# Small matmuls in blocks behind the weight units, and contractions filled up to 128 rows, in a two-layer decoder trunk

## What is computed

```python
h = rms_norm(x, norm1_g); proj = h @ w_in          # q,k,v,gates of three branches
log_a = log_sigmoid(ga @ gla_a_up + gla_a_b) / 16  # ga has 16 columns (LOWRANK)
# per chunk of 32 tokens (prompt) or per sequence of 8 (sample), for 4 GLA and 4 retention heads:
scores = where(causal, q_dec @ k_dec.T, 0)
o = q_dec @ S + scores @ v
S = exp(b_last) * S + k_end.T @ v                   # state update
# memory attention, 4 heads of 128 over 256 rows: the prompt shares one memory, each sample has its own cache
o_xa = softmax(q @ mem_k.T / sqrt(128)) @ mem_v
merged = sum(gate_b * (o_b @ w_br_b)); x = x + merged @ w_out
x = x + (gelu(conv(a)) * b) @ w_down                # a, b = h2 @ w_up
```

## Time and profile before

| | us |
|---|---|
| median of 3 runs | 1315.72 |
| the profiled execution, its own time | 1318.94 |
| span of that execution, first to last instruction | 1317.1 |
| TensorE matmul busy | 1273.7 (97% of the span) |
| GpSimd busy | 762.4 (58%) |
| VectorE busy | 641.3 (49%) |
| ScalarE busy | 578.5 (44%) |
| mean granted TensorE clock | 0.976 |

### The profile page before, as it was taken

One profiled execution on the slowest core, in us unless ns is written; L12 is line 12 of the kernel. 1 busy time (PEld: TensorE's weight loads), 2 busy tenths in 40 slices (PEclk: granted clock), 3 DMA queues, 4 the chain that ended last, 5 costly groups with the idle time before them and its releaser, 6 DMA issues.

```text
span 1317.1 us, 23794 instructions
## 1 busy us (share of the span) xinstructions
PE 1273.7 (97%) x8240; PEld 1213.6 (92%) x8240; DVE 641.3 (49%) x1247; ACT 578.5 (44%) x948; POOL 762.4 (58%) x592
## 2 busy tenths in 40 slices
PE   5999998999999999999999999999999999999995
PEld 5899888998999999999989988898989999999995
DVE  5252328447486653155242542547637765513533
ACT  6463224324434664344456432324424467634432
POOL 4643334434577677777675343435437767777773
PEclk9999989989999999999999999999989999999998
DMA  7644433334454454454564544334324444544551
GB/s 264 240 144 160 145 108 119 114 99 131 134 157 143 145 154 147 147 158 143 155 234 161 176 125 162 100 99 146 99 83 157 144 145 144 151 152 146 153 154 57
DMA packets 53209, 190.75 MB, mean 145 GB/s; under 512 B 6032, under 2 KB 7312, under 8 KB 52880
## 3 DMA queue, kind: packets, MB, share of 16 engines
q1 hardware_dynamic: 43632, 159.15, 39.1%
q10 hardware_dynamic: 9504, 30.56, 6.3%
HBM read 181.15 MB, written 8.53 MB: 144 GB/s over the span
## 4 chain that ended last, share of the span: by engine, by line
PE 89%; DVE 5%; DMA 2%; issue 2%; ACT 1%; POOL 1%; SPq 0%; DVEq 0%; ACTq 0%; POOLq 0%
PE bank L1020 41%; PE bank L1051 30%; PE bank L1064 6%; PE bank L1248 2%; DMA raw<-w 2%; PE bank L1151 1%; PE bank L1138 1%; PE bank L1237 1%; DVE arena L882 1%; PE bank L1267 1%; DVE arena L647 1%; POOL wlo L235 1%; DVE arena L896 1%; PE bank L1271 1%; PE bank L1260 1%
## 5 line engine op out<-in xcount | busy, mean ns | idle before, releaser
L235 POOL TENSOR_TENSOR wlo<-raw,whi 128x512 fp32r<-128x512 f32 x588 | 762.1, 1318 | 535.3 <-PE bank L1051 300.3
L270 ACT ACTIVATE whi<-raw 128x1024 fp32r<-128x1024 f32 x294 | 310.5, 1057 | 302.2 <-PE bank L1020 162.1
L1051 PE MATMUL bank<-oh,whi 128*128 128x320 f32 x848 | 284.9, 336 | 12.8 <-DVE arena L813 6.9
L1051 PE MATMUL bank<-ol,whi 128*128 128x320 f32 x848 | 282.1, 333 | 0.0
L1051 PE MATMUL bank<-oh,wlo 128*128 128x320 f32 x848 | 282.0, 333 | 0.0
L1020 PE MATMUL bank<-hh,whi 128*128 128x320 f32 x832 | 257.8, 310 | 0.4 <-DVE hl L906 0.4
L1020 PE MATMUL bank<-hh,wlo 128*128 128x320 f32 x832 | 257.1, 309 | 0.0
L1020 PE MATMUL bank<-hl,whi 128*128 128x320 f32 x832 | 257.1, 309 | 0.0
L1051 PEld LDWEIGHTS bank<-oh,whi 128*128 128x128 f32 x848 | 165.9, 196 | 20.6 <-DVE arena L813 7.4
L1051 PEld LDWEIGHTS bank<-oh,wlo 128*128 128x128 f32 x848 | 165.8, 196 | 3.9 <-issue 2.2
L1051 PEld LDWEIGHTS bank<-ol,whi 128*128 128x128 f32 x848 | 165.8, 196 | 3.4 <-issue 0.9
(11 more groups left out here) (190 smaller groups left out, 1744.2 us busy)
## 6 DMA issues: line engine op xcount, KB each, us to landing
raw<-w SPq DMA_DIRECT2D x296, 512.0 KB, 3.6
arena<-cache_k ACTq DMA_DIRECT2D x16, 512.0 KB, 5.6
arena<-cache_v ACTq DMA_DIRECT2D x16, 512.0 KB, 4.2
arena<-st_in ACTq DMA_DIRECT2D x8, 512.0 KB, 4.9
sst_out<-arena ACTq DMA_DIRECT2D x8, 512.0 KB, 2.8
con<-consts SPq DMA_DIRECT2D x1, 1288.0 KB, 13.5
x<-x_in SPq DMA_DIRECT2D x2, 640.0 KB, 10.5
arena<-mem_in SPq DMA_DIRECT2D x2, 512.0 KB, 6.5
```

Source lines behind the costliest of these rows:

```text
L235: i = pool.tensor_tensor(out=wlo[:, s % 2, h], in0=raw[:, s, h], in1=whi[:, s, h].bitcast(f32), op=ALU.subtract)
L270: nc.scalar.activation(whi[:, s, :], raw[:, s, :], ACT.Copy).then_inc(hi_ready, 1)
L1051: r = MM(o, a, b[:, k, 0:n], start=k == 0 and i == 0, stop=k == KT_ - 1 and i == 2, skip_group_check=True)
```

## The change

1. `unit` and `vunit` lose `small=`. The five sets become functions that issue all their matmuls in a row behind a unit.
2. In the loop over `p` the order on TensorE is now: first unit, chunk updates, scores, sample updates, second to fourth unit, outputs, fifth unit, and on as before. The sample updates stood in the third unit.
3. `sample_update` contracts over 128 rows: `kTm` has zeros in partitions 0 to 63, set once at the start (a new semaphore `km_zero`).
4. The low-rank product contracts over 128 rows too: ScalarE copies all 128 rows of the bank, and the matrix `par` has zeros below its 16 rows.
5. `pair_operands` is split in three. The keys of the next pair are spread over chunks before VectorE waits for the sample updates, those over batches before it waits for the outputs, and the queries are copied before the new sample states; all three stood behind the new sample states.

```diff
-                nc.scalar.activation(tmpa[0:LOWRANK, 0, :], A[U_GA % 2][0:LOWRANK, 0:T], ACT.Copy).then_inc(evac, 1)
+                nc.scalar.activation(tmpa[:, 0, :], A[U_GA % 2][:, 0:T], ACT.Copy).then_inc(evac, 1)
...
+                V.memset(kTm[0:64, e, :], 0.0).then_inc(km_zero, 1)
...
-                pair_operands(0)
+                chunk_keys(0)
+                query_operands(0)
+                batch_keys(0)
...
+                    if p < 3:
+                        chunk_keys(p + 1)
                     dve.wait_ge(us_done, lv * 4 + p + 1)
+                    if p < 3:
+                        batch_keys(p + 1)
                     dve.wait_ge(o_done, lv * 4 + p + 1)
+                    if p < 3:
+                        query_operands(p + 1)
                     for b in range(DEC_BATCH):
...
                     if p == 0:
                         silu(4)
-                    if p < 3:
-                        pair_operands(p + 1)
                     if p == 0:
                         silu(5)
...
                         r = MM(o, a, b[:, k, 0:n], start=k == 0 and i == 0, stop=k == KT_ - 1 and i == 2, skip_group_check=True)
-                        if small is not None and k * 3 + i < 23:
-                            small(k * 3 + i)
...
-                    MM(C[p][:, 0:T], par[0:LOWRANK, C_AU + p * P:C_AU + (p + 1) * P], tmpa[0:LOWRANK, 0, :], start=True, stop=True).then_inc(z_done, 1)
+                    MM(C[p][:, 0:T], par[:, C_AU + p * P:C_AU + (p + 1) * P], tmpa[:, 0, :], start=True, stop=True).then_inc(z_done, 1)
...
-                unit(U_QK + 4, oh, ol, T, small=lambda i: sample_scores(0, i))
-                unit(U_QK + 5, oh, ol, T, small=lambda i: sample_scores(2, i))
+                unit(U_QK + 4, oh, ol, T)
+                sample_scores(0)
+                unit(U_QK + 5, oh, ol, T)
+                sample_scores(2)
...
-                    vunit(U_RV + i, i, oh, ol, toks, RB, lambda n: sample_values(2 * i, n))
+                    vunit(U_RV + i, i, oh, ol, toks, RB)
+                    sample_values(2 * i)
...
+                def sample_updates(p):
+
+                    pe.wait_ge(ktm_ready, lv * 8 + 2 * p + 2)
+                    for i in range(DEC_BATCH):
+                        j, e = i // 2, i % 2
+                        h = 2 * (p % 2) + e
+                        r = MM(B[2 + j // 2][:, (j % 2 * 2 + e) * P:(j % 2 * 2 + e + 1) * P], kTm[:, e, j * P:(j + 1) * P],
+                               vt[:, p // 2, 2, h * P:(h + 1) * P], start=True, stop=True, skip_group_check=True)
+                    r.then_inc(us_done, 1)
...
                 for p in range(4):
                     u = U_SIL + 8 * p
+                    gated(u)
+                    if p == 0:
+                        pe.wait_ge(kt_ready, lv * 4 + 4)
+                        pe.wait_ge(v_ready, lv * 6 + 6)
+                    chunk_updates(p)
+                    scores(p)
+                    sample_updates(p)
                     gated(u + 1)
+                    gated(u + 2)
+                    gated(u + 3)
                     pe.wait_ge(s_ready, lv * 8 + 2 * p + 2)
                     pe.wait_ge(st_s[p % 2], lv * 32 + 16 * (1 + p // 2))
                     pe.wait_ge(scm_ready, lv * 16 + 4 * p + 4)
+                    outputs(p)
                     gated(u + 4)
```

More of the change, by code:

```diff
@@ L828, in pair_operands, with batch_keys @@
                                             op=ALU.mult).then_inc(ktc_ready, 1)
+                def batch_keys(p):
+                    for e in range(2):
                         V.tensor_tensor(out=kTm[64:128, e, :].rearrange("p (b k) -> p b k", k=DK),
@@ L1040, in wait_bank, with unit @@
                     pe.wait_ge(x_ready, l[0] * 24 + 24 + u - U_OUT - 1)
-            def unit(u, xh, xl, n, first_wait=None, small=None):
+            def unit(u, xh, xl, n, first_wait=None):
                 wait_bank(u)
@@ new lines, in sample_values @@
+                def sample_values(b0):
+                    for b in range(b0, b0 + 2):
+                        pe.wait_ge(cache_s[b % 4], lv * 64 + 16 * (3 + b // 4))
+                        for h in range(4):
+                            o = h * 64 + b * 8
+                            for m in range(2):
+                                r = MM(C[1][:, o:o + 8], cache[:, b % 4, m * 512 + h * P:m * 512 + (h + 1) * P],
+                                       pT[:, 0, m, b * 32 + h * 8:b * 32 + h * 8 + 8], start=m == 0, stop=m == 1, skip_group_check=True)
@@ L1187, in _ @@
                 turn(3)
[L1188 removed]
+                unit(U_QK + 6, oh, ol, T)
+                sample_scores(4)
                 rot(0)
[L1190 removed]
+                unit(U_QK + 7, oh, ol, T)
+                sample_scores(6)
                 pv(2)
@@ L1242, in sample_update @@
[L1242 to L1251, removed]
@@ L1281, in _, with scores @@
+                def scores(p):
                     pe.wait_ge(qz_ready, lv * 8 + 2 * p + 2)
@@ new lines, in outputs @@
+                def outputs(p):
+                    for a in range(2):
+                        for e in range(2):
+                            h = 2 * (p % 2) + e
+                            t0 = e * SEQ + a * P
+                            MM(C[0][:, t0:t0 + P], vt[:, p // 2, a, h * P:(h + 1) * P], scm[:, t0:t0 + P],
+                               start=a == 0 and e == 0, stop=False, skip_group_check=True)
+                    for e in range(2):
+                        h = 2 * (p % 2) + e
+                        t0 = 2 * SEQ + e * NS
+                        MM(C[1][:, e * NS:(e + 1) * NS], vt[:, p // 2, 2, h * P:(h + 1) * P], scm[:, t0:t0 + NS], start=e == 0, stop=False,
+                           skip_group_check=True)
+                    for c in range(1, NCH):
+                        MM(heads(C[0][:, :])[:, :, c * CHUNK:(c + 1) * CHUNK], S[:, c - 1, :], qz[:, :, c * CHUNK:(c + 1) * CHUNK],
+                           start=False, stop=c == NCH - 1, skip_group_check=True)
+                    for b in range(DEC_BATCH):
+                        r = MM(heads(C[1][:, 0:2 * NS])[:, :, 8 * b:8 * b + 8], s0[:, p % 2, b, :], qz[:, :, SEQ + 8 * b:SEQ + 8 * b + 8],
+                               start=False, stop=b == 7, skip_group_check=True)
+                    r.then_inc(o_done, 1)
@@ L1291, in _ @@
+                pe.wait_ge(qz_zero, 2)
+                pe.wait_ge(km_zero, 2)
+                for p in range(4):
+                    u = U_SIL + 8 * p
+                    gated(u)
[5 more added lines that the diff above has]
+                    sample_updates(p)
                     gated(u + 1)
-                    pe.wait_ge(ktm_ready, lv * 8 + 2 * p + 2)
```

85 lines of the change are left out of this document (21 added, 64 removed).

## The result

The changed kernel takes 1287.57 us (median of 4 runs, 1282.97 to 1288.36) against 1316.05 us before: a ratio of 0.9771, interval 0.975 to 0.9792, 28.5 us less. The forecast was 1278, the range 1257 to 1302. The measured time lies inside, 9.6 us above the forecast. The profiled execution is the fastest of the four, 1282.97 us; the other three lie within 1 us of each other at 1288, with a mean TensorE clock of 0.972 or 0.973 against 0.976 in the profile. So the others have more time at the low level, and where the clock falls differs a little from one execution to the next.

A forecast was written before the change was run, and what follows sets the result against it. TensorE was taken to bound the kernel (matmul in flight 97% of the span). Gains 24.8 + 23.8 + 6.9 + 0.5 + 0.4, less 1.6, gave 1264.1 profiled, 1261 median; plus 17 for clock falls, 1278 us (chance 0.48), range 1257 to 1302.

The forecast's parts named there:

- Row count of the sample updates: Sample updates on TensorE: 64 matmuls drop from 0.757 to 0.370 us each, 24.8 us gained.
- Low clock: Stretches at 1.2 GHz, mostly in third units: 51.21 us at half speed, less 1.8 overlap, 23.8 us gained.
- VectorE's new order: Keys and queries ahead of sample states: two `silu` waits go, 6.9 us gained; new square sum waits cost 1.6.
- rival (d): Late query copies at 2.74 us delay the square sum in six places: 8.7 us more, 1287 us, chance 0.06.
- Blocks: Small matmuls moved behind units cost 0.222 instead of 0.223 us: 0.5 us gained; low-rank product 0.2 a layer, 0.4.
- Sum without falls: Profiled execution with all gains and new waits but no clock falls from the blocks: 1318.9 less 54.8, 1264.1 us.
- What the blocks do to the clock: Narrow blocks on TensorE: ten low stretches, half of 16 blocks and a quarter of 8, cost 17 us; bounds 0 and 41.
- (a): The clock holds in the blocks, as passes follow without idle time: 1261 us, chance 0.30.
- Rival (b): Each of the 24 sparse blocks makes the clock fall once: 41 us more, 1302 us, chance 0.10.
- (c): Slower: the blocks themselves run at the low clock level, 83 us lost, 1344 us, chance 0.04.
- (e): The sample updates' 0.39 us belongs to something other than row count and stays: 1309.5 us, chance 0.02.
- The sign: The whole kernel gets faster by more than 2.6 us: chance 0.94; within 0.02, slower 0.04.

The follow-up runs named there:

- rows128: The kernel before with only the sample updates contracting over 128 rows with zeros, still inside the third unit of each pair: 1276.59 us, ratio 0.9684.
- block64: The changed kernel with the sample updates contracting over 64 rows, still in their block: 1292.02 us, ratio 0.9828.
- dve_order: The kernel before with only VectorE's program of the change, without the memset: 1327.85 us, ratio 1.0084.
- out_in: The changed kernel with the outputs alone back inside the fourth unit: 1299.45 us, ratio 0.9863.
- wide: The changed kernel with each sample score moving its 8 columns up to 16 times over, fewer near the bank's end: 1276.45 us, ratio 0.9682.

## Why the prediction was right or wrong

**Row count of the sample updates**, 24.8 us: right. The pair fell from 0.757 to 0.37 inside a unit, and to 0.214 a matmul in a block. `rows128` alone gives 39 us, this and the clock together. `block64` shows what the 0.39 us are: the passage into the other row count and back. Inside a unit each single matmul pays it, in a block eight pay it together.

**Low clock**, 23.8 us: right for the old places; `rows128` has no fall behind the sample updates. Its size was a little too high: the forecast has all run at half speed there, but a unit matmul goes from 0.147 to 0.267. Worked out for each form of matmul from its distances at both levels, the loss is an estimated 22.4 us before the change, and 23.7 instead of 25.6 for the 51.16 us after it.

**VectorE's new order**, 6.9 us gained and 1.6 us of new waits: right in sign and nearly in size. The new wait is 0.1 us in the first pair and none in the others, because the two query copies took 0.67 together, not 1.29. The keys ended 0.7 us behind the outputs, as the forecast expected of the first pair, but the quick copies made it good. Its 0.2 for the second pair doesn't follow from its own numbers: 1.29 + 5.78 = 7.07 against 7.04 is under 0.1. That the outputs block is the cover for this was stated, not priced. `dve_order` and `out_in` show the price, 17.5 us of waiting in two places of 8.8. Something like rival (d) is what happens without the cover. In the changed kernel it didn't happen, so that its 1287 is what was measured is a coincidence.

**Blocks**, 0.5 us: right. A narrow matmul costs 0.223 in a block, with what the next unit pays, and 0.223 inside. The low-rank product gained 0.38 us a layer instead of 0.2: it too paid for going from one row count to the other, which I had not counted.

**Sum without falls.** The profiled execution, 1283.0, less 23.7 us for its time at the low level gives 1259.3. The forecast's 1264.1 becomes 1265.5 with 22.4 us for the clock, so 6.2 us are to be found. 1.3 are the waits that were counted and didn't come, 0.4 the low-rank product. 1.0 are two waits of TensorE of 0.5 us ahead of the first unit of the loop, which the change removed and the forecast had not counted:

```profile
PE bank L1051 <- issue: 1.0, 2, 0.5
```

They stood at 170.96 and 812.02; TensorE's waits after the change have no such row. Of the other 3.5, 1.4 is a wait of TensorE for ScalarE's copy of the low-rank input, 1.6 us before and 0.2 after; between the other kernels it varies from 0.4 to 1.5, so this is not put down to the change. The rest, 2 us, isn't traced.

**What the blocks do to the clock**, 17 us: the step that failed in size. Ten stretches of 3.4 us were taken; the profile has thirteen, two of them double, 51.16 us or 23.7 us lost. Ten of the 16 narrow blocks had one (half were taken), three of the 8 outputs blocks (a quarter were taken), and I had not counted that a fall can last twice as long. So the term was 7 us too small in the profiled execution, and more in the others: the median lies 4.6 us above it at a lower mean clock. The bound of 41 us held. That half and a quarter of the blocks would fall was a guess, as the forecast said.

**From 1278 to 1287.6.** The work without falls came out 4.8 us shorter than 1264.1, the falls cost 6.7 more than 17, and the median lies 4.6 above the profiled execution where the forecast had it 3.2 below, as before the change. -4.8 + 6.7 + 4.6 + 3.2 = 9.7, the difference to rounding. So two errors in opposite directions made the number look better than its largest uncertain term was.

**Rivals.** (a) is out: the clock falls though TensorE has no idle time. The Trainium skill, TensorE: Matmul & The Clock Gate, section HAM oscillation, names idle gaps as the cause; the stretch at 107.39 begins inside a block with TensorE busy throughout (6.83 of 6.83), TensorE had no idle time in the 289.4 us around it, and `wide` removes five of seven times 3.4 us with no less idle time. Rival (b), a fall for every sparse block, is out too: 13 of 24 had one in the profile. (c) didn't happen: in most cases the unit behind the block pays, not the block. (e) is out by `rows128` and the low-rank product.

The sign was right, but its reason is in one of the five parts of the change: the zeros in the sample updates alone give 39 us, the whole 28.5. The other parts together cost 11 us.

## What to carry to other kernels

Keep all neighbouring matmuls at one row count, with zeros if need be: 64 rows cost nothing less than 128, and each passage to another count and back cost 0.39 us here. Don't collect narrow matmuls in runs of several microseconds: dealt out between wide ones, or in runs half as long, they took the same time each, and TensorE stayed at 2.4 GHz there. And before a block is dissolved or made, see what another engine does in its shadow: here the same new order of VectorE left no wait with the outputs block, where there had been 6.9 us, and cost 12 us without it. What it is worth with the block was read from the waits, not tested by a run of its own.

## What the runs showed of the hardware that I had not expected

Moving up to sixteen times the columns made the kernel 11 us faster: a pass takes 0.109 us with 8 and with 128 columns (32 passes in 3.49 us), and only behind the narrow ones did the clock fall. And VectorE's copy of 64x320 took between 0.33 us (two in 0.67) and 1.33 us (two in 2.67) each, with GpSimd idle or at work, while its operations that read a bank took 0.36 us in both cases (16 in 5.78 or 5.79).
